# The second expert phase's loads begun by two queues in turn

## The chip, the cores and the metric

The kernel runs on one core of one Trainium2 chip. The metric is device time in microseconds (us), from one launch to its end; lower is better. The other cores are idle. A profile is one further execution of the same program, recorded by the hardware profiler.

## The reference, cut to what matters

The program computes two transformer-like blocks for 256 tokens of width 1024 in f32. The change lies at the end of the first block, in the product-key expert layer. Each token picks 8 x 16 of 16,384 experts; each expert is one row of `expert_u` and one row of `expert_v`:

```python
u = expert_u[ii]
h = jnp.einsum('tkd,td->tk', u, xx).astype(f32)
a = (jax.nn.gelu(h) * gg).astype(x.dtype)
return jnp.einsum('tk,tkd->td', a, expert_v[ii])
```

What follows it is a normalisation and the second block: a gated feed-forward, a mixing layer, a second feed-forward.

## The kernel before

Two ways of computing the expert layer run side by side. For 160 of the 256 tokens (`TD`) all experts are computed densely: all of `expert_u` and then all of `expert_v` is streamed from memory, 64 MB each, and the tokens' gates are held in a big matrix `G` that is zero for experts not picked. For the other 96 tokens (`SPARSE`) only the picked rows are fetched: GpSimd issues an indirect DMA (L671) for each of 96 picks, which brings 128 rows of 4 KB; 96 of `expert_u` first, 96 of `expert_v` after that, into a ring of 6 buffers (`BUFS`). VectorE consumes each: a dot product (L2072), later a weighted sum into `XROWS` (`row_sum`, L2079 to L2094). Each consumed buffer counts in the semaphore `row_used`, on which GpSimd's next fetch into that buffer waits.

The stream is cut into items of 1 MB, 128 partitions by 8 KB, in a ring of 3 slots (`raw`, `RING`). Items of the expert stream are numbered j = 0 to 127: 0 to 63 are the first phase (`expert_u`, TensorE L1005), 64 to 127 the second (`expert_v`, TensorE L1056). In the second phase one item is two chunks c; for each, TensorE makes 8 matmuls (16 in the trace, where an f32 matmul has two records) and then counts `a_used` up by one, so an item has 32 records. The first product of an item waits until its DMA has landed (`slot_ready`, one semaphore for each slot). The item j can be begun when item j - 3, which had its slot, has been used: `a_used` at least 2 * (j - 3) + 2 - 128.

All of the stream is issued by SyncE on one queue, in order, by `load` (L594), which waits for the slot and then starts the DMA (L598). After the last expert item SyncE issues a 0.5 MB load of a gain, `FG` (L619), and then begins the items of the first feed-forward, `ffa`, under the same rule of three slots (`stream`, L603).

ScalarE has little to do in the second phase. When its last gelu of the picked rows is done (L1541), it waits until 65 rows of the second half have been summed, copies two 32-partition pieces of `XROWS` (L1544) and counts `tails_moved`; VectorE waits for that when it has begun its row 80 (L2224). ScalarE then waits until all 96 rows have been summed (`row_used`, L1546). Only then does it round the first weights of the feed-forward (`split_to`, L551) into buffers in which gathered rows had lain, loads a table, and copies the expert layer's result out of PSUM (L1551). TensorE, at the end of its products, waits for all 96 rows as well (L1059), adds them (L1064), and its result goes to that copy.

Of the kernel before, what the change touches and what calls it, by code (L numbers as in the profile page):

```python
# [7 lines left out]
P = 128  # L8
T, D = 256, 1024
NT, NK = T // P, D // P  # L10
RING = 3
# [7 lines left out]
SPARSE = 96  # L19
# [4 lines left out]
BESIDE = 3 * GROUPS  # L24
LATE = P - FIRST - BESIDE
BUFS = 6
EARLY_BANK = (4, 5, 2, 3)
PICKS = SPARSE
NEG = -3.0e38
# [18 lines left out]
EXP0 = 2 * len(PANELS1)  # L48
# [151 lines left out]
ITEM_SLOT = [i % RING for i in range(ITEMS)]  # L200
# [7 lines left out]
def before_in(ring, n):  # L208

    return next((m for m in range(n - 1, -1, -1) if ring[m] == ring[n]), None)  # L210
# [49 lines left out]
def program(nc, x, panels1, experts, peer_u, peer_v, ffa, panels2, ffb, cols, conv_cols, w_low, w_gate_up, w_sgu, k12,  # L260
# [4 lines left out]
    ACT = mybir.ActivationFunctionType  # L265
# [4 lines left out]
    with ctx:  # L270
        def sb(name, shape, dt=f32):
            return ctx.enter_context(nc.sbuf_tensor(name, shape, dt))

        def sem(name):
            return ctx.enter_context(nc.semaphore(name))


        raw = sb("raw", [P, RING, ITEM])
# [25 lines left out]
        def col(name, k=0):  # L304
            a, n = COLS[name]
            k = k % n if n == 1 else k
            assert k < n
            return C[:, a + k:a + k + 1]
# [46 lines left out]
        XROWS = Cut(cut.at)(3, D)  # L355
# [72 lines left out]
        slot_ready = [sem(f"slot_ready{s}") for s in range(RING)]  # L428
# [21 lines left out]
        xrow_ready, xrows_ready, sel_made = sem("xrow_ready"), sem("xrows_ready"), sem("sel_made")  # L450
        row_here = [sem(f"row_here{s}") for s in range(BUFS)]
        row_used, row_gelu, dots_done = sem("row_used"), sem("row_gelu"), sem("dots_done")
        turned_first, turned_second, tails_moved = sem("turned_first"), sem("turned_second"), sem("tails_moved")
# [4 lines left out]
        h_done, gelu_done, a_used = sem("h_done"), sem("gelu_done"), sem("a_used")  # L458
# [32 lines left out]
        def t_bank(stage, j):  # L491
            return ps[:, T_BANK[T_AT[stage] + j]]
# [81 lines left out]
        @block.sync  # L574
        def _(sp):
            for tt in range(NT):
                sp.dma_start(X[:, tt, :], x[0, P * tt:P * tt + P, :]).then_inc(x_in[tt], 16)
            sp.dma_start(C[:, 0:NCOLS], cols[:, 0:NCOLS]).then_inc(cols_in, 16)
            sp.dma_start(FINAL, cols[:, NCOLS:NCOLS + 8]).then_inc(cols_in, 16)
            sp.dma_start(WL, w_low).then_inc(low_in, 16)  # L580

            def wait_item_used(item):

                n = item - EXP0
                if n < 0:
                    sp.wait_ge(part_lo, 2 * item + 2)
                elif n < P // 2:
                    sp.wait_ge(h_done, 2 * n + 2)
                elif n < P:
                    sp.wait_ge(a_used, 2 * n + 2 - P)  # L590
                else:
                    sp.wait_ge(part_lo, 2 * (item - P) + 2)

            def load(item, src):  # L594
                before = before_in(ITEM_SLOT, item)
                if before is not None:
                    wait_item_used(before)
                sp.dma_start(raw[:, ITEM_SLOT[item], :], src).then_inc(slot_ready[ITEM_SLOT[item]], 16)  # L598

            for j in range(EXP0):  # L600
                load(j, panels1[j])

            def stream(item0, count, src, split0):  # L603

                for j in range(RING):
                    load(item0 + j, src[j])
                turns = (count - RING) // RING
                with sp.Fori(0, turns, 1) as i:
                    for s in range(RING):

                        sp.wait_ge(part_lo, i * (2 * RING) + (split0 + 2 * s + 2))
                        slot = ITEM_SLOT[item0 + s]
                        sp.dma_start(raw[:, slot, :], src[i * RING + (RING + s)]).then_inc(slot_ready[slot], 16)
                for j in range(RING * (turns + 1), count):
                    load(item0 + j, src[j])

            for j in range(P):
                load(EXP0 + j, experts[j])
            sp.dma_start(FG, row_post[0:1, :].broadcast_to([P, D])).then_inc(final_in, 16)  # L619
            stream(FFA0, FFI, ffa, S_FFA)  # L620
            for j in range(FFB0 - MIX0):
                load(MIX0 + j, panels2[j])
            stream(FFB0, FFI, ffb, S_FFB)
            for tt in range(NT):
                sp.wait_ge(x_piece, 8 + 2 * tt + 1)
                sp.dma_start(out[0, P * tt:P * tt + P, 0:512], X[:, tt, 0:512]).then_inc(out_done, 16)
            sp.wait_ge(out_done, 16 * 2 * NT)
# [3 lines left out]
        def _(pool):  # L631
# [36 lines left out]
            for n in range(2 * PICKS):  # L668
                if n >= BUFS:
                    pool.wait_ge(row_used, n - BUFS + 1)  # L670
                pool.indirect_dma_start(  # L671
                    out=GATHERED[n % BUFS], out_offset=None, in_=(peer_u, peer_v)[n // PICKS][:, :],
                    in_offset=bass.IndirectOffsetOnAxis(ap=ROWS[:, n % PICKS:n % PICKS + 1], axis=0))\
                    .then_inc(row_here[n % BUFS], 16)

# [23 lines left out]
        def _(pe):  # L699
# [301 lines left out]
            def hidden(n, out):  # L1001

                w = expert_in(n).rearrange("p (k e) -> p k e", k=NK)
                for k in range(NK):
                    last = pe.matmul(out[:, 0:TD], w[:, k], XF[:, k, :], start=k == 0, stop=k == NK - 1)  # L1005
                last.then_inc(h_done, 1)

            pe.wait_ge(xf_ready, 1)
            for n in range(FIRST):
                if n == 2:  # L1010
                    read_out(pe, "sc7")
                if n >= 4:
                    pe.wait_ge(gelu_done, n - 3)
                hidden(n, ps[:, EARLY_BANK[n % 4]])

# [269 lines left out]
        def _(act):  # L1285
# [182 lines left out]
            for k in range(NK):  # L1468
                if k % 2 == 0:
                    t_read_wait(act, T_AT["n2"] + k // 2)  # L1470
                last = act.activation(XF[:, k, :], t_bank("n2", k // 2)[:, T * (k % 2) + SPARSE:T * (k % 2) + T], ACT.Copy,
                                      scale=col("norm2", k))
# [11 lines left out]
            def early_gelu(n):  # L1484
                act.wait_ge(h_done, n + 1)
                act.activation(G[:, n, :], ps[:, EARLY_BANK[n % 4], 0:TD], ACT.Gelu_apprx_tanh).then_inc(gelu_done, 1)

            for n in range(FIRST):
                early_gelu(n)
                if n == FIRST // 5:  # L1490
# [4 lines left out]
                    for m in range(3):  # L1495
                        last = act.activation(XROWS[SPARSE:P, m, :], XROWS[32 * m:32 * m + 32, 0, :], ACT.Copy)
# [41 lines left out]
            for i in range(PICKS // 32):  # L1538
                act.wait_ge(dots_done, i + 1)
                c = slice(32 * i, 32 * i + 32)  # L1540
                act.activation(HS[:, c], HS[:, c], ACT.Gelu_apprx_tanh).then_inc(row_gelu, 1)  # L1541
            act.wait_ge(row_used, PICKS + 65)
            for m in range(2):
                last = act.activation(XROWS[32 * m:32 * m + 32, 0, :], XROWS[SPARSE:P, m, :], ACT.Copy)  # L1544
            last.then_inc(tails_moved, 1)
            act.wait_ge(row_used, 2 * PICKS)  # L1546
            split_to(S_FFA + 2)
            warm_root(1)
# [136 lines left out]
            for r in range(4):  # L1685
                split_to(S_AV + r + 2 + max(r - 1, 0))
                act.wait_ge(att_max, r + 1)
                for i in range(4 * r, 4 * r + 4):
                    g = i % 4
                    for tt, seg in enumerate((slice(0, P), slice(P, 384))):  # L1690
                        last = act.activation(PR[:, r, g, seg], PR[:, r, g, seg], ACT.Exp, bias=AMAX[:, i, tt:tt + 1],
                                              accum_out=ASUM[:, i, tt:tt + 1])
# [59 lines left out]
        def _(dve):  # L1752
# [305 lines left out]
            def gathered(n):  # L2058

                dve.wait_ge(row_here[n % BUFS], 16 * (n // BUFS + 1))  # L2060
                return GATHERED[n % BUFS]
# [613 lines left out]
```

## Time and profile before

| | |
|---|---|
| time, median of 3 runs | 1439.56 us (1438.53 to 1441.51) |
| the profiled execution's own time | 1436.72 us |
| its span, first to last instruction | 1435.0 us |
| mean granted TensorE clock | 0.995 |
| TensorE matmul busy | 1392.3 us, 97% of the span |
| VectorE, ScalarE, GpSimd busy | 1021.2, 522.1, 272.7 us |
| moved by DMA | 372.11 MB, 259 GB/s over the span |

The second expert phase lies from about 576 to 864 us of the span. An engine is busy while it executes an instruction; the time in which it waits for a semaphore is idle. The DMA share says how much of the time the core's 16 DMA engines were moving packets; it can come out a little above 1 by rounding. Matmuls are pipelined, so that their busy times overlap a little: the pace is read from starts, not from the mean duration.

### The profile page before, as it was taken

The numbers are of one execution on the slowest core, as the hardware profiler recorded it, in microseconds if no ns is written. First come the engines' busy times: TensorE is split into PE (matmuls) and PEld (weight loads), VectorE is DVE, ScalarE is ACT, GpSimd is POOL, SyncE is SP. The second block draws the span as 40 slices with busy tenths as digits, with TensorE's granted clock in tenths as the row PEclk, the third lists the DMA queues.
The fourth block names the chain that finished last, engine by engine and source line by source line (L and its number), as shares of the span: only waits on it lengthen the run. The fifth ranks groups of instructions, "written<-read, shape, count | busy, mean of one in ns | idle before, by whom it ended". The sixth has DMA issues, their size and how long they took to land.

```text
span 1435.0 us, 22949 instructions
## 1 busy us (share of the span) xinstructions
PE 1392.3 (97%) x8968; PEld 1278.8 (89%) x8968; DVE 1021.2 (71%) x1836; ACT 522.1 (36%) x953; POOL 272.7 (19%) x235
## 2 busy tenths in 40 slices
PE   7999999999999999999999998999999999999998
PEld 6788789999999999999999997888879978788886
DVE  5566747989888886444444437788789897687887
ACT  5545464311433332000000006444457586544444
POOL 0000036334255454333333300000000000000000
PEclk9999999999999999999999999999999999999999
DMA  6445444699999999999999984554444333455552
GB/s 234 177 147 178 171 152 161 214 412 409 371 368 377 371 363 400 405 415 416 416 413 416 415 343 171 203 201 177 176 162 167 128 103 115 165 196 199 181 199 88
DMA packets 67210, 372.11 MB, mean 259 GB/s; under 512 B 7969, under 2 KB 8481, under 8 KB 34866
## 3 DMA queue, kind: packets, MB, share of 16 engines
q1 hardware_dynamic: 37440, 266.45, 49.0%
q0 software_dynamic: 27648, 100.68, 18.0%
q10 hardware_dynamic: 2034, 3.76, 0.7%
q8 instruction: 61, 1.00, 0.3%
q14 instruction: 27, 0.22, 0.0%
HBM read 369.81 MB, written 1.05 MB: 258 GB/s over the span
## 4 chain that ended last, share of the span: by engine, by line
PE 67%; DVE 14%; DMA 10%; ACT 6%; issue 3%; POOL 0%; DVEq 0%; SPq 0%; ACTq 0%; POOLq 0%
PE ps L746 26%; PE ps L1056 12%; PE ps L779 11%; DMA raw<-in_experts 9%; PE ps L1005 9%; PE ps L781 5%; ACT xt_plain L1512 3%; DVE hi_plain L2072 2%; DVE wlo L568 2%; DVE xt_plain L2186 2%; DVE lo_plain L2072 2%; DVE arena L2175 1%; PE ps L778 1%; DVE XT L1882 1%; DVE arena L2497 1%
## 5 line engine op out<-in xcount | busy, mean ns | idle before, releaser
L1056 PE MATMUL ps<-arena,raw 128*128 128x160 f32 x2048 | 282.0, 300 | 6.6 <-DMA raw<-in_experts 6.5
L1056 PEld LDWEIGHTS ps<-arena,raw 128*128 128x128 f32 x2048 | 278.6, 190 | 9.9 <-issue 6.2
L1005 PE MATMUL ps<-arena,raw 128*128 128x160 f32 x2048 | 284.4, 300 | 2.6 <-DMA raw<-in_experts 1.3
L1005 PEld LDWEIGHTS ps<-arena,raw 128*128 128x128 f32 x2048 | 279.2, 190 | 5.1 <-DVE arena L2181 1.9
L779 PE MATMUL ps<-XT,whi 128*128 128x512 f32 x704 | 251.9, 402 | 2.2 <-DVE XT L1882 1.4
L551 ACT ACTIVATE whi<-raw 128x1024 fp32r<-128x1024 f32 x152 | 159.7, 1060 | 237.4 <-PE ps L746 109.6
L568 DVE TENSOR_TENSOR wlo<-raw,whi 128x1024 fp32r<-128x1024 f32 x138 | 167.2, 1221 | 81.1 <-ACT whi L551 80.1
L746 PE MATMUL ps<-whi,XT 128*128 128x512 f32 x592 | 185.3, 394 | 2.5 <-DVE wlo L568 1.3
L781 PE MATMUL ps<-XT,wlo 128*128 128x256 f32 x616 | 174.2, 283 | 0.0
L1606 ACT ACTIVATE whi<-raw 128x1024 fp32r<-128x1024 f32 x96 | 101.9, 1062 | 155.7 <-PE ps L779 101.6
L779 PEld LDWEIGHTS ps<-XT,whi 128*128 128x128 f32 x704 | 130.8, 190 | 29.1 <-issue 1.8
L2349 DVE TENSOR_TENSOR wlo<-raw,whi 128x1024 fp32r<-128x1024 f32 x96 | 117.3, 1222 | 44.4 <-ACT whi L1606 44.4
L746 PEld LDWEIGHTS ps<-whi,XT 128*128 128x128 f32 x592 | 109.7, 188 | 30.0 <-issue 4.0
L781 PEld LDWEIGHTS ps<-XT,wlo 128*128 128x128 f32 x616 | 117.8, 191 | 3.3
L746 PE MATMUL ps<-XT,whi 128*128 128x256 f32 x640 | 117.2, 285 | 2.8 <-DVE wlo L568 1.1
L746 PE MATMUL ps<-wlo,XT 128*128 128x512 f32 x296 | 115.6, 390 | 0.0
L2093 DVE SCALAR_TENSOR_TENSOR arena<-hi_plain,arena 128x1024 f32<-128x1024 f32 x46 | 59.1, 1285 | 76.2 <-DMA hi_plain<-in_peer_v,arena 76.2
L2093 DVE SCALAR_TENSOR_TENSOR arena<-lo_plain,arena 128x1024 f32<-128x1024 f32 x47 | 60.4, 1285 | 67.4 <-DMA lo_plain<-in_peer_v,arena 66.8
L746 PEld LDWEIGHTS ps<-XT,whi 128*128 128x128 f32 x640 | 99.5, 191 | 3.9 <-issue 1.9
L746 PE MATMUL ps<-XT,wlo 128*128 128x256 f32 x320 | 90.5, 283 | 0.0
L671 POOL DMA_INDIRECT hi_plain<-in_peer_u,arena x48 | 68.3, 1422 | 104.5 <-DVE arena L2072 76.2
L671 POOL DMA_INDIRECT lo_plain<-in_peer_u,arena x48 | 61.0, 1271 | 62.0 <-DVE arena L2072 51.9
(310 smaller groups left out, 1841.3 us busy)
## 6 DMA issues: line engine op xcount, KB each, us to landing
raw<-in_experts SPq DMA_DIRECT2D x128, 1024.0 KB, 8.0
raw<-in_panels SPq DMA_DIRECT2D x58, 1024.0 KB, 4.8
raw<-in_ffa SPq DMA_DIRECT2D x33, 1024.0 KB, 4.8
raw<-in_ffb SPq DMA_DIRECT2D x33, 1024.0 KB, 4.8
arena<-in_row_post ACTq DMA_DIRECT2D x4, 512.0 KB, 4.9
X<-in_x SPq DMA_DIRECT2D x2, 512.0 KB, 5.8
hi_plain<-in_peer_u,arena POOLq DMA_INDIRECT x48, 9.1
lo_plain<-in_peer_u,arena POOLq DMA_INDIRECT x48, 10.0
```

What stands on the lines that cost most here:

```text
L551: act.activation(whi[:, buf(p), :], half(item_of(p), p % 2), ACT.Copy).then_inc(part_hi, 1)
L568: eng.tensor_tensor(low_weights(p), half(item_of(p), p % 2), whi[:, buf(p), :].bitcast(f32), ALU.subtract).then_inc(part_lo, 1)
L671: pool.indirect_dma_start(out=GATHERED[n % BUFS], out_offset=None, in_=(peer_u, peer_v)[n // PICKS][:, :], in_offset=bass.IndirectOffsetOn ...
L746: last = pe.matmul(out, x if w_moving else w, w if w_moving else x, start=start and n == 0, stop=stop and n == 2)
L779: last = pe.matmul(out, wh[:, k], XT[:, k], start=k == 0, stop=k == NK - 1)
L781: pe.matmul(out[:, T:], wl[:, k], XTh[:, k], start=False, stop=False)
L1005: last = pe.matmul(out[:, 0:TD], w[:, k], XF[:, k, :], start=k == 0, stop=k == NK - 1)
L1056: last = pe.matmul(t_bank("ffa", k // 2)[:, at:at + TD], w[:, P * k:P * k + P], G[:, c, :], start=False, stop=False, skip_group_check=True)
L1606: act.activation(whi[:, buf(q), :], half(item_of(q), q % 2), ACT.Copy)\
L2072: dve.tensor_tensor_reduce(u, u, XROWS[:, k // 32, :], 1.0, 0.0, ALU.mult, ALU.add, HS[:, k:k + 1])\
L2093: ins = dve.scalar_tensor_tensor(into, v, a, into, ALU.mult, ALU.add)
L2349: dve.tensor_tensor(wlo[:, buf(q), :], half(item_of(q), q % 2), whi[:, buf(q), :].bitcast(f32), ALU.subtract).then_inc(part_lo, 1)
```

## The change

The items j = 69, 71, ..., 127 are left out of SyncE's loop and issued by ScalarE on its own DMA queue, each after the same wait on `a_used` as before. SyncE keeps 0 to 68 and 70, 72, ..., 126. ScalarE's two copies of `XROWS` and their wait now stand behind its issue of item 115. Sizes, slots, semaphores and what is computed stay.

```diff
+ACT_LOADS = range(P // 2 + 5, P, 2)
+TAILS_AT = 115
@@ SyncE
             for j in range(P):
-                load(EXP0 + j, experts[j])
+                if j not in ACT_LOADS:
+                    load(EXP0 + j, experts[j])
@@ ScalarE
-            act.wait_ge(row_used, PICKS + 65)
-            for m in range(2):
-                last = act.activation(XROWS[32 * m:32 * m + 32, 0, :], XROWS[SPARSE:P, m, :], ACT.Copy)
-            last.then_inc(tails_moved, 1)
+            for j in ACT_LOADS:
+                slot = ITEM_SLOT[EXP0 + j]
+                act.wait_ge(a_used, 2 * (j - RING) + 2 - P)
+                act.dma_start(raw[:, slot, :], experts[j]).then_inc(slot_ready[slot], 16)
+                if j == TAILS_AT:
+                    act.wait_ge(row_used, PICKS + 65)
+                    for m in range(2):
+                        last = act.activation(XROWS[32 * m:32 * m + 32, 0, :], XROWS[SPARSE:P, m, :], ACT.Copy)
+                    last.then_inc(tails_moved, 1)
             act.wait_ge(row_used, 2 * PICKS)
```

## Rows read from the trace of the kernel before

**Rows 1.** Busy time by stretch: us, then each engine, PEclk, DMA share, GB/s
```profile
575.80:600.00 24.20, 24.01 (x177) 23.77 (x177) 11.03 (x9) 0.00 (x0) 9.57 (x9) 1.00 1.01 402
600.00:700.00 100.00, 97.89 (x713) 96.77 (x712) 46.01 (x37) 0.00 (x0) 34.78 (x35) 1.00 1.02 415
700.00:800.00 100.00, 97.62 (x711) 96.34 (x710) 44.22 (x36) 2.11 (x2) 33.84 (x34) 1.00 1.02 415
```

**Rows 2.** Chain that ended last, beginning of the phase: start, us, what
```profile
576.00 8.71 PE ps L1056 x64
584.73 8.81 DMA raw<-in_experts
```

**Rows 3.** TensorE and weight loads in time order: start, us, instructions [idle before]
```profile
607.46 35.23 PE L1056 MATMUL ps<-arena,raw 128*128 128x160 f32 x256 [0.57 <-DMA raw<-in_experts]
643.39 35.34 PE L1056 MATMUL ps<-arena,raw 128*128 128x160 f32 x256 [0.70 <-DMA raw<-in_experts]
629.38 13.07 PEld L1056 LDWEIGHTS ps<-arena,raw 128*128 128x128 f32 x96 [0.16 <-DMA raw<-in_experts]
864.29 1.92 PE L1064 MATMUL ps<-arena 128*128 128x96 f32 x16
```

**Rows 4.** Tile raw from 575.8 to 864.4
```profile
L1056 PE MATMUL ps<-arena,raw x2048: 299/299/403, 575.8 to 864.2; 128*128 128x160 f32 x187
...
  DMA raw<-in_experts: 10.2, 18
who waited for it (us, times):
...
  PE ps L1056: 6.5, 12
  PEld ps L1056: 3.7, 6
...
DMA to landing us min/median/max: 4.7/8.1/9.5
```

**Rows 5.** DMA queues, 600 to 820 us: packets, MB, share of 16 engines
```profile
q1 hardware_dynamic: 7021, 51.10, 56.0%
q0 software_dynamic: 10990, 40.00, 45.4%
q8 instruction: 13, 0.21, 0.4%
```

**Rows 6.** The same, 696.5 to 699.5 us
```profile
q1 hardware_dynamic: 103, 0.84, 68.1%
q0 software_dynamic: 108, 0.38, 31.4%
```

**Rows 7.** The same, 708.6 to 709.2 us
```profile
q0 software_dynamic: 66, 0.24, 99.5%
q1 hardware_dynamic: 15, 0.00, 1.4%
```

**Rows 8.** The same, 704.5 to 704.9 us
```profile
q1 hardware_dynamic: 2, 0.00, 0.3%
```

**Rows 9.** Page, DMA issues: KB each, us to landing
```profile
raw<-in_panels SPq DMA_DIRECT2D x58, 1024.0 KB, 4.8
arena<-in_row_post ACTq DMA_DIRECT2D x4, 512.0 KB, 4.9
X<-in_x SPq DMA_DIRECT2D x2, 512.0 KB, 5.8
```

**Rows 10.** DMA, 832 to 848 us
```profile
DMA packets 1009, 5.73 MB, mean 358 GB/s; under 512 B 118, under 2 KB 118, under 8 KB 502
```

**Rows 11.** All engines in time order, 755 to 869 us, lines picked
```profile
761.82 1.29 DVE L2093 SCALAR_TENSOR_TENSOR arena<-lo_plain,arena 128x1024 f32<-128x1024 f32 x1
806.33 1.22 DVE L2226 TENSOR_TENSOR arena<-arena 64x1024 f32<-64x1024 f32 x1
847.10 4.67 SPq L598 DMA_DIRECT2D raw<-in_experts  x2
847.26 1.28 DVE L2093 SCALAR_TENSOR_TENSOR arena<-lo_plain,arena 128x1024 f32<-128x1024 f32 x1 [1.17 <-DMA lo_plain<-in_peer_v,arena]
855.79 9.02 SPq L598 DMA_DIRECT2D raw<-in_ffa  x3
861.43 2.00 ACT L551 ACTIVATE whi<-raw 128x1024 fp32r<-128x1024 f32 x2 [97.56 <-issue]
865.20 1.06 ACT L551 ACTIVATE whi<-raw 128x1024 fp32r<-128x1024 f32 x1 [1.77 <-DMA raw<-in_ffa]
866.28 1.28 ACT L1373 ACT_TABLE_LOAD   x1
867.68 1.07 ACT L1551 ACTIVATE arena<-ps 128x512 f32<-128x512 f32 x2
```

**Rows 12.** ScalarE in time order
```profile
574.42 0.23 ACT L1541 ACTIVATE arena<-arena 128x32 f32<-128x32 f32 x1 [0.81 <-DVEq L2076]
761.75 2.12 ACT L1544 ACTIVATE arena<-arena 32x1024 f32<-32x1024 f32 x2 [187.10 <-DVE arena L2091]
889.92 0.33 ACTq L1570 DMA_DIRECT2D arena<-in_row_post  x1
```

## The prediction

> **What bounds the kernel now.** I read the page's slices first. TensorE's clock is full nearly throughout, and its matmuls are busy for nine tenths and more of most slices; the slices from about 215 to 850 us also show the DMA engines full. The change touches only the second expert phase, so I went to the stretches of that phase [rows 1]: TensorE is 97.6 to 97.9% busy, the 16 DMA engines are at 1.02, and together they move 415 GB/s. Two things are at their limit at once, and the question is which of them ends the waits. ScalarE is idle there.
>
> The pace without a wait comes from the chain: 64 matmul records, two items, in 8.71 us, so 4.355 us for an item [rows 2]. 64 items would take 278.7 us; from the phase's first matmul at 575.8 to the product behind its last at 864.3 it takes 288.5 us [rows 3, 4]. So 9.8 us are lost, and this is all that a better feed of the second phase can give.
>
> The instructions in time order say how they are lost: not a little with every item, but in bursts, about 0.6 to 0.9 us each eight items (256 records to the next DMA wait), with a shorter one between them [rows 3]. A load may take from its issue to its landing two items, 8.71 us, before TensorE waits. The median is 8.1 and the longest 9.5 us [rows 4], while a load of the same size beside no gathers lands in 4.8 us [rows 9].
>
> **Why a load takes 8.1 us.** Over 220 us SyncE's queue (q1) moved 51.10 MB, which in packets of 8 KB is 6238, and took 56.0% of 16 engines: 0.316 us a packet. The gathers' queue (q0), 40.00 MB in packets of 4 KB, took 0.164 us a packet [rows 5]. (The rest of the packets are the small ones of semaphores and descriptors.) Where both queues have work, packets go about one for one, 103 against 108, and the stream gets 0.84 MB in 3 us, 280 GB/s [rows 6]: an item needs 8 packets on each engine, 8 x (0.316 + 0.164) = 3.84 us. But between items there is a pause in which q1 moves nothing but semaphore writes and the gathers take everything: 0.4 us in one place, 0.6 us in another [rows 7, 8]. With 0.5 us an item costs the queue 3.84 + 0.5 = 4.34 us, against the 4.355 us in which TensorE uses one. The single queue is just fast enough and has nothing to catch up with. So whatever disturbs one engine stays in the queue: a block of instructions of 16 KB, 13 in 220 us, takes 0.4% of 3520 engine-us, 1.08 us of one engine [rows 5]. It comes every 17 us, four items, and the stalls have the spacing of one or two of them. That the pause belongs to the change of item within one queue is my reading; the rows show only that it is there.
>
> **The change, part by part.**
>
> 1. *The queue.* With every second item on ScalarE's queue, each queue has 8.71 us for an item for which it needs 4.34 us of service. The pause of one queue no longer delays the item behind. The landing time should become that of an undisturbed load: 4.8 us, of which 8 x 0.316 = 2.5 us is transfer, so 2.3 us is start and receipt [rows 5, 9]; with gathers alongside 2.3 + 3.84 = 6.1 us, and up to 1 us more, since a start also competes with the gathers; I take 7.0 us. The margin to 8.71 grows from 0.6 to 1.7 us, more than the 1.08 us of an instruction block. Bounds: at best every stall goes, -9.8 us; at worst none does, 0 (or it gets worse, which is a rival below). The two queues overlap when one is late, and then a packet of the other comes between; I leave 2 us of stalls, so -7.8 us at the end of TensorE's products: 856.5 us.
>
> 2. *Issue.* 30 DMA starts leave SyncE and come to ScalarE. On ScalarE one took 0.33 us [rows 12]; it has nothing else to do and all 30 are covered by that idleness. ScalarE is free at 574.65 us, before the first of them (item 69) can start, when item 66 is used, 576 + 3 x 4.36 = 589 us. Landing from ScalarE's queue is in rows of 0.5 MB only, 4.9 us against SyncE's 5.8 us [rows 9]; so I take the same start time, between 0.9 us less and, as the unknown side, 1 us more, which the margin still holds.
>
> 3. *The copies of XROWS.* They move from 761.75 us to behind the issue of item 115. That one waits for item 112, the 49th: 576 + 49 x 4.36 = 790 us, up to 796 at the old pace. The 65 rows they wait for are there at 762 [rows 11, 12], 772 at a slower gather, so ScalarE does not block and the copies end at 792 to 798 us. Item 117 can't start before 799 us. VectorE wants them at the row before 806.3 us [rows 11], later if gathers slow. Cost nothing, cover 8 us or more; if the cover were gone, VectorE and then the fetches behind it would wait for the difference.
>
> 4. *The gathers.* A faster stream takes its bytes from them: 1.049 MB in 4.355 us is 241 GB/s instead of 232, and of 415 GB/s there remain about 173 instead of 182 [rows 1, 5], 5% less. Their last row is summed at 848.54 us [rows 11], so from 576 at this pace 5% is 14 us: about 862 us, and this would eat the gain. But the stream ends earlier too. Counted in bytes: before, at 848 us, all gathers and all items but the last two are in, and 16 us moved 5.73 of 6.64 MB, so 2.2 us were unused [rows 10]. To have everything in, add two items, 2 x 1.049 MB at 415 GB/s = 5.05 us, and the 0.5 MB of `FG`, which now follows item 126 directly and no longer item 127: 1.3 us. 848 - 2.2 + 5.05 + 1.3 = 852 us, and up to 2.5 us more if the first `ffa` item comes in before the last gather. With the last row's 1.28 us: summed at 853.4 to 855.9 us. TensorE ends at 856.5. So the gathers stop just short of being last.
>
> 5. *What is late next.* ScalarE begins its rounding only after the last row, and before its copy at L1551 it needs 2.00 + 1.06 + 1.28 us and a few tenths, 4.5 us [rows 11]: from 855.9, 860.4 us at the latest. The other way is the second `ffa` item, issued when item 126 is used, one item before TensorE's end, and landing 5.1 us later; now the rounding that waits for it starts at 865.20, 0.9 us after TensorE's end, and the copy at 867.68, 3.4 us after it. From 856.5 that is 859.9. Both ways lie about 7.5 us before the 867.68 of now. The rest of the kernel follows unchanged.
>
> The sum is -7.5 us: 1436.72 becomes 1429.2 us for the profiled execution. That execution lay 2.8 us below the median of the runs; against the median I predict 1439.56 - 7.5 = 1432.1 us.
>
> **Rivals.** *No gain, 1439.6 us.* The engines are full [rows 1], and a landing may be late because 16 shared engines are late, not because of a pause in a queue; then the same stalls come on two queues. For it: the share of 1.02, and the burst-like stalls which an instruction block causes whatever the queue. Against it: q1's pauses [rows 7, 8], in which the gathers take a bandwidth that the stream should have. The Trainium skill speaks against the change here: "DMA: Bandwidth & Descriptors", section "Issuing engines are not separate DMA queues", says that transfers begun by different engines run on the same 16 engines and that starting them from several saves only the sequencer's time. By that rule the gain would be nothing. The trace agrees that the sequencer's time is not short.
>
> *The gathers become last, 1435.9 us.* With packets of two stream queues against one of theirs they fall behind whenever both have work, and if the stream is early they get the bandwidth only at the end. If their last row is summed at 859.5 us in place of 855.9, ScalarE's copy comes 4.5 us later, at 864.0: -3.7 us. It decides from a last row at 855.5 us on.
>
> *The two items hold each other up, 1448 us, slower.* In one queue the item that TensorE wants first has all of the stream's share; in two, both share. Fully overlapped an item would need 8 x (0.316 + 0.316 + 0.164) = 6.4 us of service, 2.5 more, and land at 7.0 + 2.5 = 9.5 us, 0.8 after it is wanted. If a third of this remained in the mean, 0.3 us for each of some 60 items, 18 us of stalls would stand in place of 9.8: +8 us. It decides from landings of 8.9 us in the mean. Against it: with 3.84 us of service every 4.355 the overlap does not last once it is there, since what is late on one queue is caught up while the other rests.
>
> That ScalarE blocks at its `row_used` wait I count here too: by part 3 it has some 18 us.
>
> **How the numbers follow.** Forecast 50%, no gain 22%, gathers last 16%, slower 12%. About 0.2%, 2.9 us, is what a measurement of this kernel can tell from no change. The forecast, nearly all of it, and most of the gathers' case are faster: 0.64; no gain, with the rest of these, 0.25; slower 0.11. The forecast's own range is 1429 to 1435 us. The whole reaches from 1428.5, all stalls gone (1439.56 - 9.8 = 1429.8) and as much below as the fastest run lay under the median, to 1441, no gain with the spread of the runs.
>
> **What would show it.** Landings of `raw` with a median near 7 us and SyncE's and ScalarE's queues with about half of the stream's bytes each; TensorE's waits for `in_experts` from 10.2 us (6.5 and 3.7, matmuls and weight loads) down to 2 [rows 4]; the product at L1064 at about 856.5 us; the last row sum near 855 us, after 848.5 now; the row sums about 5% further apart; the copies of XROWS at about 790 us with no wait of VectorE behind them. The prediction is wrong if landings stay at 8 us (the pause was not the cause), if TensorE ends early but the copy at L1551 does not (the gathers), or if stalls come with every item (sharing).

## The result: slower by 0.17%

Over 20 runs of each kernel the changed one takes 1440.89 us in the median, the one before 1438.44 us; the ratio is 1.0017, 95% interval 1.0010 to 1.0024. The forecast was 1432.1 us. The profiled execution took 1437.4 us, with a span of 1435.7 us, and a second one of the same kernel had a span of 1441.8 us. So single executions differ by more than the effect. The phase itself is the better place to look, though it too differs from one profile of a kernel to the next, by some 3 us, as the experiments show.

The landings, and who waited for them, in the changed kernel (tile raw, 575.8 to 870 us; compare [rows 4]):

```profile
L600 SPq DMA_DIRECT2D raw<-in_experts x31: 327/328/328, 581.3 to 850.5; - x31
L1548 ACTq DMA_DIRECT2D raw<-in_experts x30: 334/334/335, 590.0 to 854.8; - x30
...
  DMA raw<-in_experts: 14.2, 18
...
  PE ps L1059: 8.9, 12
  PEld ps L1059: 5.2, 6
...
DMA to landing us min/median/max: 4.8/8.0/9.6
```

The loads are divided as intended, and a start costs ScalarE what it costs SyncE, 0.33 us. But the median landing is 8.0 us and not 7.0, and TensorE waits 14.2 us for `in_experts`, where it waited 10.2. The phase shows the loss, up to the product behind it (L1067 now, the L1064 of [rows 3]), in the instructions in time order:

```profile
608.15 22.00 PE L1059 MATMUL ps<-arena,raw 128*128 128x160 f32 x160 [0.70 <-DMA raw<-in_experts]
...
681.05 17.65 PE L1059 MATMUL ps<-arena,raw 128*128 128x160 f32 x128 [0.98 <-DMA raw<-in_experts]
...
845.87 21.97 PE L1059 MATMUL ps<-arena,raw 128*128 128x160 f32 x160 [1.08 <-DMA raw<-in_experts]
867.68 1.92 PE L1067 MATMUL ps<-arena 128*128 128x96 f32 x16
```

From the first product at 576.75 us to 867.68 are 290.9 us, 2.5 more than the 288.5 before. That the medians also differ by 2.45 us is in part chance: in this pair of profiles the spans differ by 0.7 us only, as some of the delay is made good behind the phase. The waits are not more, 18 in both profiles; they are longer, 0.8 us each in place of 0.6. (The spacing of eight items, which I read from [rows 3], holds only early in the phase; later waits came after three, five, nine or four items before the change too.) From 600 to 820 us (compare [rows 5]) the engines moved as much as before, 415 GB/s, but the stream got 50.45 MB in place of 51.10 and the gathers 40.68 in place of 40.00:

```profile
q0 software_dynamic: 11177, 40.68, 46.1%
q1 hardware_dynamic: 3472, 25.28, 27.7%
q10 hardware_dynamic: 3456, 25.17, 27.6%
q8 instruction: 12, 0.20, 0.4%
```

Why the landing did not shorten can be read in a stretch after ScalarE has begun a load at 698.74 us. The first three lines are the queues from 698.8 to 702.1 us and that load, the next three the queues from 702.2 to 705.6 us:

```profile
q1 hardware_dynamic: 109, 0.77, 56.5%
q0 software_dynamic: 162, 0.59, 44.6%
...
raw<-in_experts ACTq DMA_DIRECT2D x1, 1024.0 KB, 8.0
...
q10 hardware_dynamic: 123, 1.01, 71.2%
q0 software_dynamic: 118, 0.43, 31.8%
q1 hardware_dynamic: 1, 0.00, 0.0%
```

ScalarE's queue (q10) has no line in the first stretch: for 3.3 us after its start the load moves nothing, although nothing else is on that queue. Then its 1.01 MB come in 3.4 us, with SyncE's queue empty. So the two queues work in turns, just as one did, and the pause that I had put down to the queue is the start time of the load itself. It isn't a wait for the item on the other queue either. SyncE began a load at 612.79 us; the packets of the item before it, on ScalarE's queue, had ended by 614.7, and from 614.8 to 616.1 us the gathers had all engines to themselves:

```profile
q0 software_dynamic: 144, 0.52, 100.4%
q10 hardware_dynamic: 3, 0.00, 0.1%
```

### The profile page after: what moved, and what is told of

Same layout as the page of the kernel before. It is cut to its first block, busy times and chain, and to the rows that moved or that the text cites. A ratio compares the mean times of both kernels' runs of the same rounds, so it can differ in the third digit from the quotient of the medians.

```text
span 1435.7 us, 22949 instructions
## 1 busy us (share of the span) xinstructions
PE 1390.5 (97%) x8968; PEld 1276.5 (89%) x8968; DVE 1021.2 (71%) x1836; ACT 522.0 (36%) x953; POOL 280.2 (20%) x235
## 4 chain that ended last, share of the span: by engine, by line
PE 66%; DVE 14%; DMA 11%; ACT 6%; issue 3%; POOL 0%; DVEq 0%; SPq 0%; ACTq 0%; POOLq 0%
PE ps L749 26%; PE ps L1059 11%; PE ps L782 11%; DMA raw<-in_experts 10%; PE ps L1008 9%; PE ps L784 5%; ACT xt_plain L1515 3%; DVE hi_plain L2080 2%; DVE wlo L570 2%; DVE xt_plain L2194 2%; DVE lo_plain L2080 2%; DVE arena L2183 1%; DVE XT L1890 1%; PE ps L781 1%; ACT whi L553 1%
```

## Experiments

Each ratio is against the kernel before on the same chip. "The phase" is the time from the first product of the second expert phase to the product behind it (L1064 before), in the profiled execution.

**The copies moved, the queue not** (`move_only`).

```diff
+            act.wait_ge(a_used, 98)
             act.wait_ge(row_used, PICKS + 65)
```

> All loads stay on SyncE's queue; only ScalarE's two copies of XROWS come later (ScalarE waits for a_used 98 first). Theory A (the two queues themselves cost, through late packets that share an engine with the next item's): the move is free, time within 0.1% of before, waits of TensorE for in_experts 10 us as before. Rival B (the moved part of ScalarE's work costs): 1.001 to 1.002 as in the changed kernel, with a wait of VectorE before its row 80.

Ratio 1.0002 (0.9990 to 1.0015); phase 286.8 us, waits of 8.9 us for `in_experts`. VectorE's use of the copies, at 805.70 us, has no wait before it. The move costs nothing that can be measured. The wait by which rival B would act isn't there, and it falls.

**One queue, but ScalarE's** (`act_only`, `act_only_again`).

```diff
+ACT_LOADS = range(P // 2 + 5, P)
+            sp.wait_ge(a_used, 122)
             sp.dma_start(FG, ...)
```

> Items 69 to 127 all on ScalarE's queue, none on SyncE's; FG at its old place (SyncE waits for a_used 122). One queue again, but the other one. Theory A (alternating queues cost): 1.000 to 1.001, TensorE's waits for in_experts about 10 us. Rival C (ScalarE's queue is the slower one, or its issue comes later): landings above 8.2 us for all items, waits of 14 us or more, ratio 1.002 to 1.004.

> All of items 69 to 127 on ScalarE's queue again, since 1.0008 with an interval of 0.9996 to 1.0021 left both open. Theory A: 0.999 to 1.001. Rival C (ScalarE's queue is the slower one): 1.001 to 1.002.

Ratios 1.0008 (0.9996 to 1.0021) and 1.0011 (1.0000 to 1.0023); phases 290.1 and 289.3 us, waits of 13.2 and 11.5 us. The first ratio is within the range of theory A and the second just above it. The landings, 8.1 us in the median of the first, are not above SyncE's. A cost of ScalarE's queue of up to 0.1% is neither shown nor excluded.

**Without the gathers of `expert_v`**, on one queue and on two (`no_v_rows_one`, `no_v_rows_two`).

```diff
-            for n in range(2 * PICKS):
+            for n in range(PICKS):
...
-                dve.wait_ge(row_here[n % BUFS], 16 * (n // BUFS + 1))
+                if n < PICKS:
+                    dve.wait_ge(row_here[n % BUFS], 16 * (n // BUFS + 1))
```

> Left out: the gathers of expert_v; the row sums run on what lies in the buffers. All loads on SyncE's queue. Theory D (the landing of 8 us is made by the gathers on the same engines): landings about 5 us in the second phase, no waits of TensorE for in_experts, the phase 278.7 + 0.5 us long from the first L1056 to L1064. Rival E (a load takes 8 us because of the queue's own order or of the memory): landings stay above 7 us.

> The same with the alternating queues; left out: the gathers of expert_v. Theory D: the same landings of about 5 us and the same length of the phase as with one queue, within 0.3 us: without the gathers the number of queues changes nothing. Rival C (ScalarE's queue is slower): ScalarE's landings 0.5 us or more above SyncE's.

One queue: TensorE in time order, and the queues and landings from 600 to 820 us:

```profile
577.07 278.35 PE L1056 MATMUL ps<-arena,raw 128*128 128x160 f32 x2048
855.26 1.92 PE L1064 MATMUL ps<-arena 128*128 128x96 f32 x16
```

```profile
q1 hardware_dynamic: 7305, 53.29, 68.6%
q8 instruction: 13, 0.21, 0.4%
...
raw<-in_experts SPq DMA_DIRECT2D x50, 1024.0 KB, 4.8
```

Two queues:

```profile
576.41 278.35 PE L1059 MATMUL ps<-arena,raw 128*128 128x160 f32 x2048
854.60 1.92 PE L1067 MATMUL ps<-arena 128*128 128x96 f32 x16
```

All 2048 records follow one another without a wait, and the phase takes 278.2 us in both. The instruction blocks are still there, 13 in 220 us, and do no harm when a load lands in 4.8 us. The times, one run each, were 1426.66 and 1429.13 us; as the phases are equal, the difference lies outside them, and single runs differ by as much. Theory D holds: the 8 us are made by the gathers, and rival E, to which my own account of the queue belongs, falls.

The packets say which part of a landing the gathers lengthen. With one queue and no gathers, SyncE began a load at 603.35 us. From 603.7 to 604.25 us no packet moves at all; from 604.25 to 607.9 us the whole item does:

```profile
q1 hardware_dynamic: 144, 1.05, 81.2%
```

Over the loads begun from 600 to 820 us the medians here are 0.96 us from issue to first packet, 3.53 from first to last packet and 0.35 from there to landing. With the gathers, in the trace of the loop with one queue below, they are 3.47, 3.82 and 0.65 us.

**TensorE's phase as a hardware loop**, on one queue and on two, each twice.

```diff
-            for c in range(P):
-                if c >= FIRST:
-                    pe.wait_ge(beside_done, c - FIRST + 1)
-                w = expert_in(P + c)
-                ... (8 matmuls with G[:, c, :])
+            for c in range(8):
+                second(expert_in(P + c), G[:, c, :])
+            pe.wait_ge(beside_done, BESIDE + LATE)
+            with pe.Fori(0, 20, 1) as i:
+                for s in range(RING):
+                    item = EXP0 + P // 2 + 4 + s
+                    wait_loaded(pe, item, i * 16)
+                    for h in range(2):
+                        second(half(item, h), arena[:, bass.ds(i * (6 * TD) + (8 + 2 * s + h) * TD, TD)])
```

> TensorE's second phase is a hardware loop (20 turns of three items, after four items written out), so that its code is fetched once and not in blocks of 16 KB every fourth item; all loads on SyncE's queue. Theory F (each stall comes from an instruction block on one DMA engine, which delays that engine's share of an item by 1.1 us while the margin is 0.6 us): the waits for in_experts fall from 10 us to under 2, the phase is 279 to 281 us instead of 288.5, less if the gathers hold the end; time -5 to -8 us, ratio 0.994 to 0.997. Rival G (stalls come from full DMA engines whatever the code does): waits stay at 8 to 10 us, ratio 0.999 to 1.001, or above 1 by the cost of 20 branches.

> The same loop with the alternating queues of the changed kernel. Theory F: with no instruction blocks there is nothing late that could share an engine with the next item, so the two queues cost nothing: within 0.1% of the loop with one queue. Rival C (two queues cost by themselves, in every item): 0.1% or more above the loop with one queue, waits of 2 us more.

> The loop of 20 turns with one queue again, for a tighter interval: 0.992 to 0.995, second phase 280 to 281 us.

> The loop with two queues again. Theory A (two queues cost only where a block has made a packet late): within 0.1% of the loop with one queue. Rival C (they cost in every item, or at the end of the phase): 0.1 to 0.3% above it, as in the first run, 1432.12 against 1428.88 us.

| | ratio | 95% interval | median us | phase us |
|---|---|---|---|---|
| loop, one queue | 0.9934 | 0.9915 to 0.9952 | 1428.88 | 280.4 |
| again | 0.9938 | 0.9925 to 0.9952 | 1429.85 | 280.1 |
| loop, two queues | 0.9966 | 0.9942 to 0.9989 | 1432.12 | 281.0 |
| again | 0.9935 | 0.9922 to 0.9949 | 1428.80 | 280.8 |

The loop with one queue, TensorE in time order:

```profile
589.43 22.00 PE L1053 MATMUL ps<-arena,raw 128*128 128x160 f32 x160 [0.61 <-DMA raw<-in_experts]
611.80 122.14 PE L1053 MATMUL ps<-arena,raw 128*128 x896 [0.38 <-DMA raw<-in_experts]
734.20 121.97 PE L1053 MATMUL ps<-arena,raw 128*128 x896 [0.25 <-DMA raw<-in_experts]
856.00 1.92 PE L1071 MATMUL ps<-arena 128*128 128x96 f32 x16
```

Its queues and landings from 600 to 820 us, and VectorE's last row sum:

```profile
q1 hardware_dynamic: 7247, 52.74, 57.8%
q0 software_dynamic: 10655, 38.79, 44.0%
q8 instruction: 1, 0.02, 0.0%
...
raw<-in_experts SPq DMA_DIRECT2D x50, 1024.0 KB, 8.0
```

```profile
851.75 1.28 DVE L2100 SCALAR_TENSOR_TENSOR arena<-lo_plain,arena 128x1024 f32<-128x1024 f32 x1 [2.00 <-DMA lo_plain<-in_peer_v,arena]
```

The engines are as full as before and a load still lands in 8.0 us; only the blocks are gone, 1 in place of 13, and with them the stalls: 2.1 us of waits in place of 10.2, runs of 28 items without one. Theory F holds and rival G falls: the block is what pushes a load beyond its margin. The kept traces of the unrolled kernels agree: in the changed kernel, blocks begin at 641.9, 660.6, 678.2 and 697.3 us, and waits of TensorE's matmuls end at 644.4, 666.8, 681.1 and 699.5, 2.2 to 6.2 us behind the start of the block before them. This version beats the kernel before by 8.5 to 9.5 us and the changed one by more. In the repeat the two queues beside the loop lie within 0.1% of one, which speaks for theory A. In the first run of both they lay 3 us above it, with intervals that overlap by 0.001 only, and that I can't explain.

**The changed kernel again, and with `FG` at its old place** (`changed_again`, `fg_last`).

```diff
+            sp.wait_ge(a_used, 122)
             sp.dma_start(FG, ...)
```

> The changed kernel once more, beside the loops on the same chip. Theory A: ratio 1.001 to 1.003, waits of TensorE for in_experts 12 us or more in the second phase, each stall behind an instruction block of 16 KB. If it comes out at 1.000 with waits of 10 us, its loss was chance.

> The changed kernel with FG begun where it was before, after item 127 (SyncE waits for a_used 122). If the 0.5 MB beside the last gathers and item 127 cost anything, this gives it back: ratio 1.000 to 1.001. Otherwise it stays at 1.001 to 1.003.

Ratios 1.0017 (1.0007 to 1.0026) and 1.0022 (1.0013 to 1.0032); phases 293.1 and 292.5 us, waits of 17.9 and 18.2 us. The loss repeats, and the place of `FG` has no part in it.

**Two queues dealt out in pairs, and the kernel before once more** (`pairs`, `before_again`).

```diff
-ACT_LOADS = range(P // 2 + 5, P, 2)
-TAILS_AT = 115
+ACT_LOADS = [j for j in range(P // 2 + 5, P) if (j - 69) // 2 % 2 == 0]
+TAILS_AT = 114
```

> Two queues, but changed after every second item (69, 70 on ScalarE's, 71, 72 on SyncE's, ...), with the copies of XROWS behind item 114. Theory A (what costs is that an item late on one engine meets the next item on the other queue): half of the hand-overs stay within a queue, so the second phase is 289 to 290.5 us, between before (287 to 288.5) and the changed kernel (291 to 293); ratio 1.0005 to 1.0015. Rival J (having the load on two queues at all costs, however it is dealt out): as the changed kernel, 291 to 293 us.

> The kernel before, unchanged, for a second profile and for what a comparison of equal kernels gives: ratio within 0.1% of 1, second phase 286.5 to 289 us. If it is 291 us, a difference between single profiles of the second phase means nothing.

Pairs: 1.0006 (0.9993 to 1.0018), phase 289.7 us. Before: 1.0007 (0.9994 to 1.0019), phase 290.1 us, above the range that I had set for it. The phases of the unrolled kernels are then, one queue of SyncE's 288.5, 286.8, 290.1; one of ScalarE's 290.1, 289.3; pairs 289.7; alternating 290.9, 293.1, 292.5 us. The three alternating ones are all above all others, by 3.7 us in the mean against SyncE's queue, by 2.5 against ScalarE's. The pairs, one profile, are not told apart from a single queue, neither by the phase nor by the ratio. So it is probably the change of queue with every item that costs, more than having two. The ratios alone don't show it: the interval of the changed kernel, 1.0010 to 1.0024, overlaps those of the pairs and of ScalarE's single queue, and even the kernel before against itself came out at 1.0007.

**Half items on the two queues** (`halves_two`; the new function alone, its callers left out).

```diff
+        def load_half(eng, j, h):
+            slot = ITEM_SLOT[EXP0 + j]
+            eng.wait_ge(a_used, 2 * (j - RING) + 1 + h - P)
+            eng.dma_start(raw[:, slot, PART * h:PART * h + PART], experts[j][:, PART * h:PART * h + PART])\
+               .then_inc((slot_ready if h else first_ready)[slot], 16)
```

> From item 69 on each item is begun as two halves of 0.5 MB, the first on SyncE's queue when the first chunk of the item three before is used, the second on ScalarE's when the second is; TensorE waits for each half. A half may then take 5 chunks, 10.9 us, to land, not 8.7. If landings stay under 9.5 us the stalls go: -5 to -8 us, unless the gathers become last (row sums end after 856 us). Against it: 4 KB packets, one for one with those of the gathers, take a smaller share: if landings exceed 10.9 us the time is above before.

Ratio 1.0037 (1.0024 to 1.0050). TensorE and VectorE in time order:

```profile
868.58 3.73 PE L1083 MATMUL ps<-arena 128*128 128x96 f32 x16 [15.24 <-DVE arena L2115]
```

```profile
864.47 4.06 DVE L2115 SCALAR_TENSOR_TENSOR arena<-lo_plain,arena 128x1024 f32<-128x1024 f32 x3
```

A half lands in 8.3 us in the median and 9.3 at most, well within its 10.9, and TensorE does not wait once for the stream, though the instruction blocks are there, 13 in 220 us. So a block stalls TensorE only where the margin is short. But it then stands 15.24 us before the rows of the gathers. Their share fell to 36.61 MB in 220 us, and all queues together moved 409 GB/s instead of 415. This is the rival "the gathers become last", reached in another way.

**Three gathers in flight** (`bufs3`).

```diff
-BUFS = 6
+BUFS = 3
```

> GpSimd keeps 3 gathers in flight instead of 6, in both halves of the picked rows; loads on one queue. Theory H (a load starts late because the engines already hold packets of several gathers): landings fall from 8.1 to 7 us or below, and the stalls with them, while the gathers stay about as fast or become slower and last. Rival I (one waiting gather is enough for the delay): landings stay at 8 us, gathers' time from issue to landing halves from 15.4 us.

From 640 to 940 us:

```profile
raw<-in_experts SPq DMA_DIRECT2D x60, 1024.0 KB, 8.1
...
hi_plain<-in_peer_v,arena POOLq DMA_INDIRECT x90, 8.8
```

The gathers' time to landing halves, that of the loads stays at 8.1 us: rival I. The gathers became so slow that the kernel took 1527.87 us, one run, and the engines were less full than before. TensorE's waits for `in_experts` were 4.5 us from 640 us on, fewer than before; why, with the same landings, isn't shown. The lateness of a load beside gathers therefore does not depend on how many stand in line, 3 or 6; what makes it stays open.

## Why the prediction was wrong

*The bound and the loss* held. 9.8 us of stalls were all there was: without gathers the phase takes 278.2 us, where 278.7 was worked out. The sign of being wrong that the prediction named first, landings that stay at 8 us, is what came.

*Why a load takes 8.1 us*: half right. The pace of 3.84 us for an item, one packet for one, is in the packets: 3.82 us from the first to the last of an item in the loop with one queue, and in the changed kernel 1.01 MB in 3.4 us, 123 packets against 118. The pause was read wrongly, as the queue's cost between items. It is the start time of the next load. The single queue was not full, and "has nothing to catch up with" was no property of it.

*Part 1, the queue*, is the step that failed: the landing time that "should become that of an undisturbed load", with up to 1 us for a start beside the gathers, 7.0 us in all. The term that was too small is the start. Without gathers the first packet comes 0.96 us after the issue, beside them 3.47, in the loop on one queue and on two: 2.5 us more and not 1. (The undisturbed 4.8 us were also split wrongly: their transfer is 3.5 us and not 2.5, so that start and receipt are 1.3 and not 2.3.) With 3.82 us of transfer and 0.65 of receipt a load beside gathers lands after 8.0 us, whatever the queue. The margin to 8.71 us stayed at 0.7 us and did not become 1.7. A block of 1.08 us, whose part in the stalls was seen rightly and is shown by the loop, still exceeds it.

*The sign.* The slower rival, that two items hold each other up, fits the runs in kind but not in size: +8 us against +2.5. It would need a late item. Undisturbed, the two queues do not overlap; after a block the late packets of one item and the first of the next would be on the same engines, where in one queue the late ones go first. That this sharing is what makes the stalls longer is argued and not shown. Shown is that the loss repeats (1.0017, again 1.0017, and 1.0022 with `FG` moved), and that two queues alternating cost 3.7 us of phase in the mean with blocks and nothing without gathers. The 0.6 to 0.7 us between the loops is less than two profiles of one kernel differ by. In the changed kernel SyncE's loads were also the later ones, 8.4 us in the median from 600 to 820 us against ScalarE's 8.0, where in the loop both took 8.0; a block comes about every fourth item, so it may meet the same queue again and again. No run tests that.

*The rival "no gain"* gave the reason why the gain stayed away: the engines are shared, and a block is late whatever the queue. The Trainium skill's sentence in "DMA: Bandwidth & Descriptors", section "Issuing engines are not separate DMA queues", weighed there against my reading of the pause, is borne out as far as the missing gain goes: by it only the sequencer's time to start a load is saved, and with 0.33 us for a start and one start each 4.355 us that was never short.

*Part 3, the copies*: right, with less cover than thought. ScalarE's copies in the changed kernel, and VectorE's use of them:

```profile
800.42 2.12 ACT L1552 ACTIVATE arena<-arena 32x1024 f32<-32x1024 f32 x2 [224.87 <-PE ps L1059]
```

```profile
804.00 1.22 DVE L2234 TENSOR_TENSOR arena<-arena 64x1024 f32<-64x1024 f32 x1
```

Done at 802.54 us, wanted at 804.00, no wait: 1.5 us of cover where 8 were claimed, since TensorE was later and the gathers did not slow down.

*Parts 4 and 5, the gathers and what is late next*, could not show in the changed kernel, where the stream did not get faster and the last row was summed at 847.5 us. In the loop they did: last row at 853.0 us with one queue and 855.0 with two, where 853.4 to 855.9 was worked out, TensorE's end at 856.0 and 856.5 where 856.5 was, and the copy out of PSUM at 861.3 and 859.6 where 860 was. The arithmetic was about right, of a change that this one was not. That it agrees to the microsecond is luck: in the repeats of the loops the last row came at 852.9 and 851.5 us, and in the second profile of the kernel before at 841.8 where the first had 848.5.

## What to carry to other kernels

A time from issue to landing has three parts, start, transfer and receipt (here 3.47, 3.82 and 0.65 us); in this kernel a second queue shortened none of them, as the first had hardly a packet left when its next load could move. Before moving loads to another queue, look whether that queue really holds two loads at once, in a stretch just after an issue. Where the margin of a load (0.7 us here) is smaller than the time that a block of instructions takes of one DMA engine (1.08 us), and the engines are full, look for a stall behind each block in a long unrolled stretch of code; here a hardware loop removed 12 of 13 blocks and nearly all stalls.

## What was not expected of the hardware

A load beside a stream of gathers lands 3.2 us later than alone (8.0 against 4.8 us). Of that only 0.3 us is the shared transfer (3.82 against 3.53) and 0.3 the receipt (0.65 against 0.35); the other 2.5 us are a later start (3.47 against 0.96). Landings are the same with 3 or 6 gathers in flight. TensorE's unrolled second phase, 2048 matmul records and as many weight loads, fetched 13 blocks of 16 KB in 220 us and lost some 8 us by it (288.5 against 280.4 us of phase); 20 turns of a loop with a computed address cost little, since the phase was within about 2 us of the 278.2 that it takes without gathers.
